# The last block of the last projection cut at columns 416 and 128, and the final norm's statistics and row scaling rearranged

## The chip, the cores and the metric

One core of a Trainium2 chip runs one launch of a hand-written program for five engines: TensorE (PE, with its weight loads PEld), VectorE (DVE), ScalarE (ACT), GpSimd (POOL) and SyncE (SP). The metric is the device time of one execution in microseconds, lower is better; the time shown is the median of several executions.

## The reference, cut to what matters

An encoder of four layers works on 512 prompt tokens and 32 sample tokens, 1024 features each. Each layer is a mixer (linear attention, band attention, a recurrent block) and a SwiGLU feed-forward network. The change touches the end alone: the second half of the last `w_out` product and the final norm.

```python
def rmsnorm(x, g):
    xf = x.astype(jnp.float32)
    y = xf * lax.rsqrt(jnp.mean(xf * xf, axis=-1, keepdims=True) + EPS)
    return (y * g.astype(jnp.float32)).astype(x.dtype)

def swiglu_ffn(x, w_in, w_out):
    g, u = jnp.split(x @ w_in, 2, axis=-1)
    return (jax.nn.silu(g) * u) @ w_out
...
        xp = xp + swiglu_ffn(rmsnorm(xp, ffn_norms[i]), *ffn_params[i])
        xs = xs + swiglu_ffn(rmsnorm(xs, ffn_norms[i]), *ffn_params[i])
    y_prompt = rmsnorm(xp, final_norm)
    y_sample = rmsnorm(xs, final_norm)
```

## The kernel before

Activations lie transposed in memory: `x` holds eight blocks (`XT` = 8) of 128 features by 544 tokens (`TOK`). Tokens 0 to 511 are the prompt, in four tiles of 128 (tiles 0 to 3), and the last 32 are the sample, tile `QT` = 4; the turn of tile 4 takes the last 128 columns and 32 rows of the result are used.

A projection makes one block of 128 output features at a time. For the last one, `down1` of layer 3, the contraction has 11 steps (`FH`), and each step is three matmuls (high times high, low times high, high times low halves of activations `h` and weights `w`), since products are split into two reduced-precision float32 parts (dtype fp32r). The name of a matmul in the rows is output, then activations and weights. Blocks 0 to 6 run in `mm_block` (lines 2378 in the rows), each matmul twice, on 272 columns. VectorE scales the block by `rstd` (L2052) and adds it to `x` (L2055); ScalarE squares it (L783) and makes a copy with the final gain, `xf` (L1236); GpSimd adds the squares into `sq_sum` (L2982); TensorE turns `xf` into token rows five tiles at a time (`end_turn`, L2337) and ScalarE copies these to `EN["rows"]` (L1219, L1220). Each of these is one block behind TensorE.

Block 7, the last, is computed in two token parts, `END_PARTS`: part 0 is columns 256 to 543 with tiles 2, 3 and 4, part 1 is columns 0 to 255 with tiles 0 and 1. TensorE's matmuls for both are at L2842 in `last_project`. For each part this chain follows:

- VectorE multiplies by `rstd` (L2059) and adds to `x` (L2062)
- ScalarE squares (L1425) and makes the copy with the gain (L1427)
- VectorE adds the squares to `sq_sum` (L2065)
- TensorE sums over the features with one matmul of one column for each tile (`end_sum`, L2860), then turns the tiles of block 7 (`end_turn_last`, L2337)
- ScalarE takes the root (L1430), VectorE the reciprocal (L2068)
- VectorE (L2074, L2076) and ScalarE (L1433, L1435) scale the rows of a tile: first 896 columns from `EN["rows"]`, then the last 128 from PSUM
- a DMA writes the tile's 128 rows of 1024 float32 (512 KB; the sample 128 KB)

Order is set by the order of the code on each engine and by semaphores; there is no scheduler. On TensorE `end_sum(0)` and `end_turn_last(0)` stand between the steps of part 1 (after steps 4 and 5). VectorE and ScalarE run all of part 0 and then all of part 1. SP issues the writes of tiles 2, 3, 4 and 0 (L735, L737, L739, L741), each behind its wait; ScalarE issues that of tile 1 last (L1438).

Of the kernel before, what the change touches and what calls it, by code (L numbers as in the profile page):

```python
# [24 lines left out]
ALU = mybir.AluOpType  # L25
# [156 lines left out]
def encoder_step(nc, d, o, layers=4):  # L182
# [15 lines left out]
    with ctx:  # L198
# [3 lines left out]
        def sem(name):  # L202
            return ctx.enter_context(nc.semaphore(name))
# [116 lines left out]
        def one(t, m, cols=slice(0, TOK), rows=slice(0, P)):  # L320
# [49 lines left out]
        s_eh, s_ea, s_esq, s_exf, s_esum, s_est, s_erms, s_einv, s_etn = (sem("end_part_" + n) for n in (  # L370
            "mm", "x", "square", "x_gain", "squares_summed", "mean_mm", "rms", "inv_rms", "turned"))
# [8 lines left out]
        END_PARTS = ((slice(2 * P, TOK), (2, 3, QT)), (slice(0, 2 * P), (0, 1)))  # L380
        END_LAST = (XT - 1) * P
        END_AT = {0: A0[:, 0:P], 2: A0[:, P:2 * P], QT: A0[:, 2 * P:3 * P], 1: A1[:, 0:P], 3: A1[:, P:2 * P]}
# [45 lines left out]
        def gain(name, m):  # L428
            return vec_a[:, ds(m + COL_A[name], 1)]
# [105 lines left out]
        def _(sp):  # L535
# [198 lines left out]
            sp.wait_ge(s_yd, 1)  # L734
            sp.dma_start(y_rows[:, 2:3, :], EN["rows"][:, 2:3, :]).then_inc(s_yo, 16)  # L735
            sp.wait_ge(s_ya, 1)
            sp.dma_start(y_rows[:, 3:4, :], EN["rows"][:, 3:4, :]).then_inc(s_yo, 16)  # L737
# [10 lines left out]
        def _(act):  # L748
# [672 lines left out]
            for c, (cols, tiles) in enumerate(END_PARTS):  # L1421
                t = tiles[1]
# [4 lines left out]
                act.activation(EN["xf"][1][:, cols], one(x, XT - 1, cols), ACT.Copy,  # L1427
                               scale=gain("final_norm", XT - 1)).then_inc(s_exf, 1)
                act.wait_ge(s_est, c + 1)
                act.activation(rms5[:, tiles[0]:tiles[-1] + 1], A2[:, 480 + tiles[0]:481 + tiles[-1]], ACT.Sqrt,  # L1430
                               bias=eps[:, 0:1]).then_inc(s_erms, 1)
                act.wait_ge(s_einv, c + 1)
                act.activation(EN["rows"][:, t, 0:END_LAST], EN["rows"][:, t, 0:END_LAST], ACT.Copy, scale=inv5[:, t:t + 1])  # L1433
                act.wait_ge(s_etn, c + 1)
                act.activation(EN["rows"][:, t, END_LAST:], END_AT[t], ACT.Copy,  # L1435
                               scale=inv5[:, t:t + 1]).then_inc(s_ya, 1)
            act.wait_ge(s_ya, 2)
            act.dma_start(y_rows[:, 1:2, :], EN["rows"][:, 1:2, :]).then_inc(s_yo, 16)  # L1438
# [5 lines left out]
        def _(dve):  # L1444
# [600 lines left out]
            def last_project(i, b0, kt):  # L2045
# [11 lines left out]
                for c, (cols, tiles) in enumerate(END_PARTS):  # L2057
# [12 lines left out]
                    dve.wait_ge(s_ye, m)  # L2070
                    for t in tiles[0:3:2]:
                        rows = ALL if t < QT else SAMPLE
                        inv = inv5[rows, t:t + 1]
                        dve.tensor_scalar(EN["rows"][rows, t, 0:END_LAST], EN["rows"][rows, t, 0:END_LAST], inv, None, ALU.mult)  # L2074
                        dve.wait_ge(s_etn, c + 1)
                        dve.tensor_scalar(EN["rows"][rows, t, END_LAST:], END_AT[t][rows, :], inv, None, ALU.mult).then_inc(s_yd, 1)  # L2076
# [256 lines left out]
        def _(pe):  # L2333
# [495 lines left out]
            def last_project(b0, q0):  # L2829
# [9 lines left out]
                for c, (cols, tiles) in enumerate(END_PARTS):  # L2839
                    for k in range(FH):  # L2840
# [14 lines left out]
            def end_sum(c):  # L2855

                pe.wait_ge(s_esum, c + 1)
                for t in END_PARTS[c][1]:
                    cols = slice(t * P, (t + 1) * P) if t < QT else slice(TOK - P, TOK)
                    ins = pe.matmul(A2[:, 480 + t:481 + t], sq_sum[:, cols], mean_x[:, 0:1], start=True, stop=True)  # L2860
                ins.then_inc(s_est, 1)

            def end_turn_last(c):

                pe.wait_ge(s_exf, c + 1)
                pe.wait_ge(s_ye, XT - 2)
# [244 lines left out]
```

## Time and profile before

| | us |
|---|---|
| median of 3 runs | 2536.77 (2536.25 to 2537.08) |
| profiled execution, its time | 2536.17 |
| its span, first to last event | 2534.4 |
| last block's first matmul, from the span's start | 2515.57 |
| last matmul of its part 1 starts | 2525.80 |
| first output write issued | 2525.04 |
| last output write issued | 2530.44 |

The page gives for each engine its busy share of the span; the chain of waits, followed back from the last event, gives what would have to be shorter for the end to come earlier. Times inside the trace count from the span's start. Only the last 19 us of the span belong to the code that the change touches.

### The profile page before, as it was taken

To read this page: it belongs to the slowest core of one execution; us is meant where nothing else is said; L and a number is where in the kernel's file an instruction comes from. 1 tells how busy PE (TensorE), PEld (TensorE's weight loads), DVE (VectorE), ACT (ScalarE), POOL (GpSimd) and SP (SyncE) were. 2 spreads that over 40 slices of the span, in tenths; PEclk is the share of its full clock that TensorE was granted. 3 is DMA by queue.
4 is the path that set the end of the run, shared out by engine and by line. 5 is a ranking of instruction groups with operands and counts; after the bars stand their busy time and mean duration, and the time that the engine had idled before them with its cause. 6 is when DMAs were issued, how large, how long until landed. Compare 5 with 4: busy or idle time off the path is not lost.

```text
span 2534.4 us, 48129 instructions
## 1 busy us (share of the span) xinstructions
PE 2516.1 (99%) x19925; PEld 2451.5 (97%) x19925; DVE 1747.4 (69%) x2578; ACT 1206.0 (48%) x1822; POOL 169.1 (7%) x180
## 2 busy tenths in 40 slices
PE   8999999999999999999999999999999999999998
PEld 8999999999988899999998899999999999999998
DVE  6555994984555599489557557948955565984973
ACT  5454651543555565245245545524534544642543
POOL 1101000001000010000122210000011101000001
PEclk9999999999999999999999999999999999999999
DMA  4222333332433233333222233332323223333332
GB/s 120 71 78 84 100 102 91 100 96 78 120 97 109 74 108 96 97 95 96 85 68 76 70 91 88 102 102 84 97 81 88 72 70 90 109 88 93 106 89 78
DMA packets 443890, 230.68 MB, mean 91 GB/s; under 512 B 17092, under 2 KB 440736, under 8 KB 443696
## 3 DMA queue, kind: packets, MB, share of 16 engines
q1 hardware_dynamic: 442048, 226.90, 31.2%
q8 instruction: 140, 2.29, 0.4%
q10 hardware_dynamic: 1200, 0.59, 0.1%
q0 software_dynamic: 448, 0.45, 0.1%
q14 instruction: 54, 0.44, 0.1%
HBM read 219.03 MB, written 8.87 MB: 90 GB/s over the span
## 4 chain that ended last, share of the span: by engine, by line
PE 96%; DVE 2%; ACT 1%; issue 1%; DMA 0%; SPq 0%; ACTq 0%; DVEq 0%
PE slot L2378 32%; PE slot L2421 21%; PE aux L2885 6%; PE aux L2880 6%; PE aux L2882 6%; PE slot L2885 5%; PE slot L2880 5%; PE slot L2882 5%; PE aux L2337 2%; PE aux L2783 1%; PE aux L2546 1%; PE aux L2789 1%; PE aux L2695 1%; PE aux L2633 1%; PE aux L2561 1%
## 5 line engine op out<-in xcount | busy, mean ns | idle before, releaser
L765 ACT ACTIVATE w_hi<-raw 128x1024 fp32r<-128x1024 f32 (+3 forms) x208 | 241.1, 1159 | 275.3 <-PE slot L2421 136.7
L2378 PE MATMUL slot<-xg_hi,w_hi 128*128 128x272 f32 x1664 | 361.4, 298 | 2.5 <-DVE w_lo L1462 1.5
L2378 PE MATMUL slot<-xg_lo,w_hi 128*128 128x272 f32 x1664 | 343.7, 288 | 0.0
L2378 PE MATMUL slot<-xg_hi,w_lo 128*128 128x272 f32 x1664 | 343.6, 288 | 0.0
L1462 DVE TENSOR_TENSOR w_lo<-raw,w_hi 128x1024 fp32r<-128x1024 f32 (+4 forms) x208 | 284.2, 1366 | 68.8 <-ACT w_hi L765 66.8
L2378 PEld LDWEIGHTS slot<-xg_hi,w_hi 128*128 128x128 f32 x1664 | 260.5, 189 | 14.2 <-issue 7.8
L2378 PEld LDWEIGHTS slot<-xg_lo,w_hi 128*128 128x128 f32 x1664 | 261.3, 188 | 0.0
L2378 PEld LDWEIGHTS slot<-xg_hi,w_lo 128*128 128x128 f32 x1664 | 260.3, 189 | 0.0
L2982 POOL TENSOR_TENSOR sq_sum<-sq_sum,sq_x 128x544 f32<-128x544 f32 x48 | 67.9, 1414 | 1609.8 <-ACT sq_x L783 1609.5
L2097 DVE TENSOR_TENSOR ffn_y<-slot,rstd 128x544 f32<-128x544 f32 x56 | 40.6, 725 | 193.9 <-PE slot L2421 177.7
L2421 PE MATMUL slot<-h_hi,w_hi 128*128 128x272 f32 x1078 | 150.0, 287 | 0.0
L2421 PE MATMUL slot<-h_hi,w_lo 128*128 128x272 f32 x1078 | 149.8, 287 | 0.0
L2421 PE MATMUL slot<-h_lo,w_hi 128*128 128x272 f32 x1078 | 149.8, 287 | 0.0
L783 ACT ACTIVATE sq_x<-x 128x544 f32<-128x544 f32 (+1 forms) x55 | 36.2, 657 | 223.0 <-DVE x L2100 119.4
L2421 PEld LDWEIGHTS slot<-h_hi,w_hi 128*128 128x128 f32 x1078 | 140.5, 188 | 0.0
L2421 PEld LDWEIGHTS slot<-h_lo,w_hi 128*128 128x128 f32 x1078 | 140.1, 188 | 0.0
L2421 PEld LDWEIGHTS slot<-h_hi,w_lo 128*128 128x128 f32 x1078 | 140.0, 188 | 0.0
L2885 PE MATMUL aux<-ffn_t_hi,w_lo 128*128 128x272 f32 x704 | 116.7, 287 | 0.0
L2880 PE MATMUL aux<-ffn_t_hi,w_hi 128*128 128x272 f32 x704 | 116.6, 287 | 0.0
L2882 PE MATMUL aux<-ffn_t_lo,w_hi 128*128 128x272 f32 x704 | 116.5, 287 | 0.0
L1290 ACT ACTIVATE w_hi<-ffn_w_sums 128x1024 fp32r<-128x1024 f32 x80 | 85.1, 1064 | 65.9 <-DVE ffn_w_sums L2134 64.8
L1308 ACT ACTIVATE w_hi<-ffn_w_sums 128x1024 fp32r<-128x1024 f32 x80 | 85.0, 1062 | 61.8 <-PE aux L2885 29.5
(406 smaller groups left out, 5757.4 us busy)
## 6 DMA issues: line engine op xcount, KB each, us to landing
raw<-in_l_ffn_w_out_dram SPq DMA_DIRECT2D x64, 704.0 KB, 4.7
raw<-in_l_ffn_w_in_dram SPq DMA_DIRECT2D x52, 512.0 KB, 5.0
raw<-in_l_gla_w_in_dram SPq DMA_DIRECT2D x47, 512.0 KB, 3.9
ffn_raw_b<-in_l_ffn_w_in_dram SPq DMA_DIRECT2D x88, 256.0 KB, 3.4
ffn_raw_b<-in_l_ffn_w_in_dram SPq DMA_DIRECT2D x44, 512.0 KB, 5.2
raw<-in_l_ffn_w_in_dram SPq DMA_DIRECT2D x72, 256.0 KB, 3.4
raw<-in_l_att_w_qkv_dram SPq DMA_DIRECT2D x24, 512.0 KB, 3.8
raw<-in_l_lru_w_in_dram SPq DMA_DIRECT2D x24, 512.0 KB, 3.9
```

The costliest lines, as they stand in the source:

```text
L765: act.activation(w_hi[par][:, 0:kt, :], raw[par][:, 0:kt, :], ACT.Copy).then_inc(s_hi, 1)
L1290: act.activation(tiles8(w_his, w_slots(b % 2)[0]), tiles8(FF["s"], 0), ACT.Copy).then_inc(s_wh, 1)
L1308: act.activation(tiles8(w_his, min(w_slots(b % 2)[2:4])), tiles8(FF["s"], 2 * KQ), ACT.Copy).then_inc(s_wh, 1)
L1462: dve.tensor_tensor(w_lo[par][:, 0:kt, :], raw[par][:, 0:kt, :], w_hi[par][:, 0:kt, :].bitcast(F32), ALU.subtract).then_inc(s_lo, 1)
L2097: dve.tensor_tensor(FF["y"][:, 2 * j:2 * j + 2, :], slot[(p0 + j) % 2][:, :, 0:HALF], halves(rstd[:, :]), ALU.mult).then_inc(s_free, 1)
L2337: return pe.transpose(out, in_, ident[rows, rows])
L2378: ins = pe.matmul((slot[par] if bank is None else bank)[:, hf, 0:HALF], w[par][:, k, :], a[:, k0 + k, hf * HALF:(hf + 1) * HALF], start=(k ...
L2421: ins = pe.matmul(to[:, hf, 0:HALF], w[par][:, k, :], a[:, k, cols], start=(k == 0 and at == 0), stop=(k == kt - 1 and at == 2))
L2880: pe.matmul(to, w_his[:, w_at + k, :], hi(k), start=(start and k == 0), stop=False, skip_group_check=True)
L2882: pe.matmul(to, w_his[:, w_at + k, :], lo(k), start=False, stop=False, skip_group_check=True)
L2885: ins = pe.matmul(to, w_los[:, w_at + k, :], hi(k), start=False, stop=(stop and k == KQ - 1), skip_group_check=True)
L2982: pool.tensor_tensor(sq_sum[:, :], sq_sum[:, :], sq_x[par][:, :], ALU.add).then_inc(s_xad, 1)
```

## The change

`END_PARTS` becomes part 0 = columns 128 to 543 with tiles 1, 2, 3 and 4, and part 1 = columns 0 to 127 with tile 0. VectorE's addition of the squares goes; `end_sum` makes two accumulating matmuls for a tile, one on `sq_sum` and one on the block's squares `sq_x[1]`. On TensorE `end_sum(0)` and `end_turn_last(0)` move from between the steps of part 1 to behind them. VectorE runs the add of part 1 right after the reciprocal of part 0, and then scales tiles 1 and 4, takes part 1's reciprocal, and scales tile 0. ScalarE scales the front of tile 2, squares part 1, finishes tile 2, takes part 1's root and scales tile 3. SP writes tiles 1, 2, 4 and 0, ScalarE tile 3.

```diff
-        END_PARTS = ((slice(2 * P, TOK), (2, 3, QT)), (slice(0, 2 * P), (0, 1)))
+        END_PARTS = ((slice(P, TOK), (1, 2, 3, QT)), (slice(0, P), (0,)))
...
             sp.wait_ge(s_yd, 1)
+            sp.dma_start(y_rows[:, 1:2, :], EN["rows"][:, 1:2, :]).then_inc(s_yo, 16)
+            sp.wait_ge(s_ya, 1)
             sp.dma_start(y_rows[:, 2:3, :], EN["rows"][:, 2:3, :]).then_inc(s_yo, 16)
-            sp.wait_ge(s_ya, 1)
-            sp.dma_start(y_rows[:, 3:4, :], EN["rows"][:, 3:4, :]).then_inc(s_yo, 16)
...
+            end_square(0)
+            end_root(0)
+            act.wait_ge(s_einv, 1)
+            end_front(2)
+            end_square(1)
+            act.wait_ge(s_etn, 1)
+            end_back(2)
+            end_root(1)
+            end_front(3)
+            end_back(3)
             act.wait_ge(s_ya, 2)
-            act.dma_start(y_rows[:, 1:2, :], EN["rows"][:, 1:2, :]).then_inc(s_yo, 16)
+            act.dma_start(y_rows[:, 3:4, :], EN["rows"][:, 3:4, :]).then_inc(s_yo, 16)
...
-                    dve.wait_ge(s_esq, c + 1)
-                    dve.wait_ge(s_xad, (XT - 2) * stat_of["final"])
-                    dve.tensor_tensor(sq_sum[:, cols], sq_sum[:, cols], sq_x[m % 2][:, cols], ALU.add).then_inc(s_esum, 1)
...
+                end_add(0)
+                end_inverse(0)
+                end_add(1)
+                dve.wait_ge(s_ye, m)
+                end_rows(0, 1)
+                end_rows(0, QT)
+                end_inverse(1)
+                end_rows(1, 0)
...
-                        if c and k == 4:
-                            end_sum(0)
-                        if c and k == 5:
-                            end_turn_last(0)
+                end_sum(0)
+                end_turn_last(0)
                 end_sum(1)
                 end_turn_last(1)

             def end_sum(c):

-                pe.wait_ge(s_esum, c + 1)
+                pe.wait_ge(s_xad, (XT - 2) * stat_of["final"])
+                pe.wait_ge(s_esq, c + 1)
                 for t in END_PARTS[c][1]:
                     cols = slice(t * P, (t + 1) * P) if t < QT else slice(TOK - P, TOK)
-                    ins = pe.matmul(A2[:, 480 + t:481 + t], sq_sum[:, cols], mean_x[:, 0:1], start=True, stop=True)
+                    pe.matmul(A2[:, 480 + t:481 + t], sq_sum[:, cols], mean_x[:, 0:1], start=True, stop=False)
+                    ins = pe.matmul(A2[:, 480 + t:481 + t], sq_x[1][:, cols], mean_x[:, 0:1], start=False, stop=True)
                 ins.then_inc(s_est, 1)
```

TensorE before, inside part 1 (L2842 are its steps, L2860 the sums of part 0 over the features, L2337 the turns of part 0's tiles):

```order
L2842 MATMUL slot<-h_hi,w_hi 128x256
L2842 MATMUL slot<-h_lo,w_hi 128x256
L2842 MATMUL slot<-h_hi,w_lo 128x256
L2860 MATMUL aux<-mean_x,sq_sum 128x1 [waits end_part_squares_summed]
L2860 MATMUL aux<-mean_x,sq_sum 128x1 x2
L2842 MATMUL slot<-h_hi,w_hi 128x256
L2842 MATMUL slot<-h_lo,w_hi 128x256
L2842 MATMUL slot<-h_hi,w_lo 128x256
L2337 MATMUL aux<-ident,end_xf 128x128 [waits end_rows,end_part_x_gain]
L2337 MATMUL aux<-ident,end_xf 128x128 x2
```

TensorE of the change, from the last matmul of part 1 on (now L2873, with 128 columns; the sums are L2890 and L2891, the turns L2368):

```order
L2873 MATMUL slot<-h_hi,w_lo 128x128
L2890 MATMUL aux<-mean_x,sq_sum 128x1 [waits end_part_square,square_added]
L2891 MATMUL aux<-mean_x,sq_x 128x1
L2890 MATMUL aux<-mean_x,sq_sum 128x1
L2891 MATMUL aux<-mean_x,sq_x 128x1
L2890 MATMUL aux<-mean_x,sq_sum 128x1
L2891 MATMUL aux<-mean_x,sq_x 128x1
L2890 MATMUL aux<-mean_x,sq_sum 128x1
L2891 MATMUL aux<-mean_x,sq_x 128x1
L2368 MATMUL aux<-ident,end_xf 128x128 [waits end_rows,end_part_x_gain]
L2368 MATMUL aux<-ident,end_xf 128x128 x3
```

Part 0's sums are now eight matmuls where there were three, and stand behind all of part 1's matmuls instead of in their middle; part 1's sums follow behind the turns.

VectorE before, part 0 from its reciprocal on and then part 1:

```order
L2068 RECIPROCAL inv<-rms 128x3 [waits end_part_rms]
L2074 TENSOR_SCALAR end_rows<-end_rows,inv 128x896 [waits end_rows,end_part_inv_rms]
L2076 TENSOR_SCALAR end_rows<-aux,inv 128x128 [waits end_part_turned]
L2074 TENSOR_SCALAR end_rows<-end_rows,inv 32x896
L2076 TENSOR_SCALAR end_rows<-aux,inv 32x128 [waits end_part_turned]
L2059 TENSOR_TENSOR ffn_y<-slot,rstd 128x256 [waits end_part_mm]
L2062 TENSOR_TENSOR x<-ffn_y,x 128x256 [waits block_read]
L2065 TENSOR_TENSOR sq_sum<-sq_sum,sq_x 128x256 [waits square_added,end_part_square]
L2068 RECIPROCAL inv<-rms 128x2 [waits end_part_rms]
L2074 TENSOR_SCALAR end_rows<-end_rows,inv 128x896 [waits end_rows,end_part_inv_rms]
L2076 TENSOR_SCALAR end_rows<-aux,inv 128x128 [waits end_part_turned]
```

VectorE of the change, the same stretch:

```order
L2090 RECIPROCAL inv<-rms 128x4 [waits end_part_rms]
L2080 TENSOR_TENSOR ffn_y<-slot,rstd 128x128 [waits end_part_mm,end_part_inv_rms]
L2083 TENSOR_TENSOR x<-ffn_y,x 128x128 [waits block_read]
L2097 TENSOR_SCALAR end_rows<-end_rows,inv 128x896 [waits end_rows]
L2099 TENSOR_SCALAR end_rows<-aux,inv 128x128 [waits end_part_turned]
L2097 TENSOR_SCALAR end_rows<-end_rows,inv 32x896
L2099 TENSOR_SCALAR end_rows<-aux,inv 32x128 [waits end_part_turned]
L2090 RECIPROCAL inv<-rms 128x1 [waits end_part_rms]
L2097 TENSOR_SCALAR end_rows<-end_rows,inv 128x896 [waits end_part_inv_rms]
L2099 TENSOR_SCALAR end_rows<-aux,inv 128x128 [waits end_part_turned]
```

Part 1's multiply and add moved ahead of all row scaling, and stand behind the reciprocal of part 0; the addition of squares is gone.

ScalarE before, and then of the change, from part 0's root on:

```order
L1430 ACTIVATE rms<-aux,eps 128x3 [waits end_part_mean_mm]
L1433 ACTIVATE end_rows<-end_rows,inv 128x896 [waits end_part_inv_rms]
L1435 ACTIVATE end_rows<-aux,inv 128x128 [waits end_part_turned]
L1425 ACTIVATE sq_x<-x 128x256 [waits square_added,end_part_x]
L1427 ACTIVATE end_xf<-x,vec_a 128x256 [waits end_turned]
L1430 ACTIVATE rms<-aux,eps 128x2 [waits end_part_mean_mm]
L1433 ACTIVATE end_rows<-end_rows,inv 128x896 [waits end_part_inv_rms]
L1435 ACTIVATE end_rows<-aux,inv 128x128 [waits end_part_turned]
L1438 DMA out_dram<-end_rows 128x1024 [waits end_scaled_act]
```

The same of the change:

```order
L1435 ACTIVATE rms<-aux,eps 128x4 [waits end_part_mean_mm]
L1440 ACTIVATE end_rows<-end_rows,inv 128x896 [waits end_part_inv_rms]
L1426 ACTIVATE sq_x<-x 128x128 [waits square_added,end_part_x]
L1428 ACTIVATE end_xf<-x,vec_a 128x128 [waits end_turned]
L1444 ACTIVATE end_rows<-aux,inv 128x128 [waits end_part_turned]
L1435 ACTIVATE rms<-aux,eps 128x1 [waits end_part_mean_mm]
L1440 ACTIVATE end_rows<-end_rows,inv 128x896
L1444 ACTIVATE end_rows<-aux,inv 128x128
L1456 DMA out_dram<-end_rows 128x1024 [waits end_scaled_act]
```

Part 1's square and gained copy moved between the two pieces of the first tile's scaling, ahead of the wait for that tile's turn.

## Rows read from the trace of the kernel before

**Rows 1.** The page's chain that ended last: its shares by engine.

```profile
PE 96%; DVE 2%; ACT 1%; issue 1%; DMA 0%; SPq 0%; ACTq 0%; DVEq 0%
```

**Rows 2.** Chain of waits, last 35 us: start us, us, what.

```profile
2504.68 8.26 PE slot L2378 x66
...
2515.73 3.20 PE slot L2842 x24
2518.93 0.55 PE aux L2337 x5
...
2520.71 0.47 DVE ffn_y L2059
...
2522.17 0.47 DVE sq_sum L2065
...
2522.68 0.84 PE aux L2860 x6
...
2523.55 0.28 ACT rms L1430
...
2524.06 0.69 DVE end_rows L2074
...
2526.13 0.44 DVE ffn_y L2059
...
2527.98 0.62 PE aux L2860 x4
...
2529.11 1.04 ACT end_rows L1433
2530.16 0.26 ACT end_rows L1435
```

**Rows 3.** Timeline of TensorE in the last block: start, duration, instruction.

```profile
2515.57 0.29 PE L2842 MATMUL slot<-h_hi,w_hi 128*128 128x288 f32 x1
...
2520.51 0.28 PE L2842 MATMUL slot<-h_hi,w_hi 128*128 128x256 f32 x1
...
2523.83 0.49 PE L2337 MATMUL aux<-ident,end_xf 128*128 128x128 f32 x3
...
2524.28 0.28 PE L2842 MATMUL slot<-h_lo,w_hi 128*128 128x256 f32 x1
...
2525.80 0.28 PE L2842 MATMUL slot<-h_hi,w_lo 128*128 128x256 f32 x1
```

**Rows 4.** Groups by shape, 2490 to 2535 us: busy us, mean ns.

```profile
L2052 DVE TENSOR_TENSOR ffn_y<-slot,rstd 128x544 f32<-128x544 f32 x4 | 2.9, 725 | 12.2 <-PE slot L2378 12.2
...
L2059 DVE TENSOR_TENSOR ffn_y<-slot,rstd 128x256 f32<-128x256 f32 x1 | 0.4, 425 | 0.0
...
L783 ACT ACTIVATE sq_x<-x 128x544 f32<-128x544 f32 x4 | 2.6, 658 | 11.5 <-DVE x L2055 11.5
...
L1427 ACT ACTIVATE end_xf<-x,vec_a 128x256 f32<-128x256 f32 x1 | 0.5, 492 | 0.0
...
L1425 ACT ACTIVATE sq_x<-x 128x256 f32<-128x256 f32 x1 | 0.4, 416 | 1.7 <-DVE x L2062 1.7
```

**Rows 5.** Timeline of the output writes' issue: start, duration, queue.

```profile
2525.04 0.36 SPq L735 DMA_DIRECT2D out_dram<-end_rows  x1
...
2530.09 0.34 SPq L741 DMA_DIRECT2D out_dram<-end_rows  x1
2530.44 0.36 ACTq L1438 DMA_DIRECT2D out_dram<-end_rows  x1
```

**Rows 6.** Stretches at the end: engines' busy us, clock share, DMA share, GB/s.

```profile
2530.00:2531.00 1.00, 0.00 (x0) 0.00 (x0) 0.06 (x1) 0.41 (x2) 0.00 (x0) 0.64 0.10 41
2531.00:2532.00 1.00, 0.00 (x0) 0.00 (x0) 0.00 (x0) 0.00 (x0) 0.00 (x0) 0.50 1.00 401
2532.00:2533.00 1.00, 0.00 (x0) 0.00 (x0) 0.00 (x0) 0.00 (x0) 0.00 (x0) 0.50 1.02 401
2533.00:2534.00 1.00, 0.00 (x0) 0.00 (x0) 0.00 (x0) 0.00 (x0) 0.00 (x0) 0.50 0.53 205
```

More of the change, by code:

```diff
@@ L369, in encoder_step @@
             "end_x_gain", "end_turned", "end_rows", "end_scaled_dve", "end_scaled_act", "y_out"))
-        s_eh, s_ea, s_esq, s_exf, s_esum, s_est, s_erms, s_einv, s_etn = (sem("end_part_" + n) for n in (
-            "mm", "x", "square", "x_gain", "squares_summed", "mean_mm", "rms", "inv_rms", "turned"))
+        s_eh, s_ea, s_esq, s_exf, s_est, s_erms, s_einv, s_etn = (sem("end_part_" + n) for n in (
+            "mm", "x", "square", "x_gain", "mean_mm", "rms", "inv_rms", "turned"))
         s_hp = sem("head_square")
@@ L379, in encoder_step @@
         END_BANKS = ((A3, A2), (A0, A1))
[L380 removed]
+        END_PARTS = ((slice(P, TOK), (1, 2, 3, QT)), (slice(0, P), (0,)))
         END_LAST = (XT - 1) * P
[L382 removed]
+        END_AT = {0: A3[:, 0:P], 1: A0[:, 0:P], QT: A0[:, P:2 * P], 2: A1[:, 0:P], 3: A1[:, P:2 * P]}
         SCORE_BANK = (A0, A1)
@@ L1420, in _, with end_square @@
             n, y_rows = stat_of["final"] - 1, o[0].rearrange("a (t p) n -> (a p) t n", p=P)
-            for c, (cols, tiles) in enumerate(END_PARTS):
-                t = tiles[1]
+            def end_square(c):
+                cols = END_PARTS[c][0]
                 act.wait_ge(s_ea, c + 1)
@@ L1428, in _, with end_root @@
                                scale=gain("final_norm", XT - 1)).then_inc(s_exf, 1)
+            def end_root(c):
+                tiles = END_PARTS[c][1]
                 act.wait_ge(s_est, c + 1)
@@ L1431, in _, with end_front, end_back @@
                                bias=eps[:, 0:1]).then_inc(s_erms, 1)
-                act.wait_ge(s_einv, c + 1)
+            def end_front(t):
                 act.activation(EN["rows"][:, t, 0:END_LAST], EN["rows"][:, t, 0:END_LAST], ACT.Copy, scale=inv5[:, t:t + 1])
-                act.wait_ge(s_etn, c + 1)
-                act.activation(EN["rows"][:, t, END_LAST:], END_AT[t], ACT.Copy,
-                               scale=inv5[:, t:t + 1]).then_inc(s_ya, 1)
+            def end_back(t):
+                act.activation(EN["rows"][:, t, END_LAST:], END_AT[t], ACT.Copy, scale=inv5[:, t:t + 1]).then_inc(s_ya, 1)
+            end_square(0)
[8 more added lines that the diff above has]
+            end_back(3)
             act.wait_ge(s_ya, 2)
-            act.dma_start(y_rows[:, 1:2, :], EN["rows"][:, 1:2, :]).then_inc(s_yo, 16)
+            act.dma_start(y_rows[:, 3:4, :], EN["rows"][:, 3:4, :]).then_inc(s_yo, 16)
         @block.vector
@@ L2056, in last_project, with end_add @@
                 m = XT - 1
-                for c, (cols, tiles) in enumerate(END_PARTS):
+                def end_add(c):
+                    cols = END_PARTS[c][0]
                     dve.wait_ge(s_eh, c + 1)
@@ L2062, in last_project, with end_inverse @@
                     dve.tensor_tensor(one(x, m, cols), FF["u"][:, cols], one(x, m, cols), ALU.add).then_inc(s_ea, 1)
-                    dve.wait_ge(s_esq, c + 1)
-                    dve.wait_ge(s_xad, (XT - 2) * stat_of["final"])
-                    dve.tensor_tensor(sq_sum[:, cols], sq_sum[:, cols], sq_x[m % 2][:, cols], ALU.add).then_inc(s_esum, 1)
+                def end_inverse(c):
+                    tiles = END_PARTS[c][1]
                     part = slice(tiles[0], tiles[-1] + 1)
@@ L2069, in last_project, with end_rows @@
                     dve.wait_ge(s_einv, c + 1)
[L2070 to L2076, printed above, removed]
+                def end_rows(c, t):
+                    rows = ALL if t < QT else SAMPLE
+                    inv = inv5[rows, t:t + 1]
+                    dve.tensor_scalar(EN["rows"][rows, t, 0:END_LAST], EN["rows"][rows, t, 0:END_LAST], inv, None, ALU.mult)
+                    dve.wait_ge(s_etn, c + 1)
+                    dve.tensor_scalar(EN["rows"][rows, t, END_LAST:], END_AT[t][rows, :], inv, None, ALU.mult).then_inc(s_yd, 1)
+                end_add(0)
[6 more added lines that the diff above has]
+                end_rows(1, 0)
             def project_out(i, name, b0, kt):
@@ L2865, in end_turn_last @@
                 pe.wait_ge(s_exf, c + 1)
-                pe.wait_ge(s_ye, XT - 2)
+                pe.wait_ge(s_ye, XT - 2 + c)
                 for t in END_PARTS[c][1]:
```

## Prediction

> **What bounds the kernel now.** First the chain by engine [rows 1]: TensorE is 96% of it, so nothing off TensorE matters until the last block. Then the chain of waits in the last 35 us [rows 2], which is where the whole change lies: the reader sees TensorE's steps, then from 2520.71 us on a relay of short pieces through VectorE, ScalarE and TensorE, once for part 0 and, from 2526.13, once for part 1, to 2530.42 (2530.16 + 0.26). Nothing in it overlaps. Then TensorE's timeline for the pace of single matmuls [rows 3], the groups by shape for how an operation's time grows with columns [rows 4], the issue times of the writes [rows 5], and the stretches at the end [rows 6]. The last shows what the chain of waits leaves out: from 2531 to 2533.5 the core does nothing but write output, at 401 GB/s with the DMA engines busy 1.00 of the time. The bandwidth of the write is the last limit, and how much is still unwritten when the last chain closes decides the end.
>
> How far the end lies behind the last data: 41 + 401 + 401 + 205 is 1.05 MB, which is the two tiles issued at 2530.09 and 2530.44 [rows 5, 6]. So data flowed from about 2530.90 (41/401 of a microsecond before 2531), 0.81 us behind the first issue, to about 2533.51 (205/401 of one behind 2533), and the span of 2534.4 ends 0.89 us later. The three other pieces (1.18 MB) were issued from 2525.04 on and had 5 us beside the chain of part 1 to drain.
>
> **TensorE, part 0: 416 columns instead of 288.** The paces in the rows are 24 matmuls of 288 columns in 3.20 us (0.133), 66 of 272 in 8.26 us (0.125) [rows 2], and 13 steps of 256 columns from 2524.28 to 2525.80 (0.117) [rows 3]. In proportion, 416 columns take 0.193; by the slope from 256 to 288 (0.5 ns for a column) 0.197; I take 0.193. 33 x (0.193 - 0.133) is +1.98 us. The turn of block 6 inside the part (0.55 [rows 2]) stays. So the multiply of part 0 moves from 2520.71 to about 2522.70, and part 1's first matmul from 2520.51 [rows 3] to 2522.49.
>
> **TensorE, part 1: 128 columns instead of 256.** No row has a fp32r matmul of 128 columns. Every matmul has its own weight load, and the nearest rows for what lies under it are the sums and the turns: the sums move one column, and 6 records take 0.84 and 4 take 0.62 us [rows 2], 0.11 for each more; the turns move 128 columns, 5 take 0.71 - the first 0.27 of it is one matmul's own length - and 3 take 0.49 [rows 3], again 0.11. Halving the columns of a one-column or a 128-column matmul buys nothing; I read 0.112 as the floor that the weight load sets. Bounds: half of 0.117, which is 0.058, if no load binds; two records of 0.112, which is 0.224, if a narrow fp32r matmul runs as the sums do (see below). I take 0.112, since fp32r and plain float32 loads have the same 128x128 weights. 33 x 0.112 = 3.70 us, and part 1 ends at 2522.49 + 3.70 = 2526.19. Before, the last matmul of part 1 started at 2525.80, with part 0's sums and turns already inside.
>
> The Trainium skill, "TensorE: Matmul & The Clock Gate", section "LDWEIGHTS (loading the stationary operand)", makes a weight load cost its columns divided by 1.2 in ns, an estimate of 107 ns for 128. The rows' 0.11 agrees, and by the page's value the sum would be 0.2 us less. What this rule says against the change: a matmul with fewer columns than its weight load hides costs its load, so cutting off a small part does not make that part cheap.
>
> **The squares.** VectorE's addition goes (0.47 of part 0's chain [rows 2], and as much in part 1's). In its place each sum has two matmuls. A sum of three tiles shows as 6 records [rows 2], two for each matmul, so part 0 now has 4 tiles x 2 x 2 = 16 records and part 1 has 4. The root followed the first record by 0.87 (2522.68 to 2523.55) with 6 and by 0.64 with 4; 16 give 0.64 + 12 x 0.112 = 1.98.
>
> **Where the sums stand.** Part 0's chain: multiply and add at 0.59 each (725 ns at 544 columns, 425 at 256, so 1.04 ns a column [rows 4]), square 0.55 (658 and 416 ns), hand-overs 0.03 each: the squares are ready at 2522.70 + 0.59 + 0.03 + 0.59 + 0.03 + 0.55 = 2524.49. Nobody takes them: TensorE is in part 1 until 2526.19. That is a wait of 1.7 us that before did not exist, since the sums stood inside part 1. The square and the gained copy are hidden by it, and so is the saved addition of part 0. Then root at 2526.19 + 1.98 = 2528.17, and from the root to the scaling 0.51 (2523.55 to 2524.06 [rows 2]): 2528.68. Before, part 0 reached this point at 2524.06: 4.6 us earlier.
>
> **Who is queued behind.** Part 1's multiply and add (0.29 each, the same line through 725 and 425) stand behind part 0's reciprocal on VectorE, though TensorE has finished part 1 at 2526.2. They run from 2528.68 to 2529.32. ScalarE is in tile 2's front from 2528.68 (1.04 [rows 2], next start 0.95 later), so the square of part 1 starts at 2529.63 and takes 0.31. TensorE's sum of part 1 starts at 2529.98, its root at 2530.62, tile 3's front at 2530.90, its back piece 0.95 later, and that ends 0.35 later: tile 3 is issued by ScalarE at about 2532.22. The gained copy (492 ns at 256 columns, about 0.39 here) and the back of tile 2 fill ScalarE until the root and cost nothing more; tile 2 is ready at about 2530.5.
> VectorE: tile 1 from 2529.34, issued 0.98 later (2524.06 to 2525.04 [rows 2, 5]) at 2530.32; the sample 1.09 later at 2531.41 (2525.04 to 2526.13); reciprocal 0.21; tile 0 issued at 2532.60.
>
> **The sum.** The last issue moves from 2530.44 to 2532.60. The first moves from 2525.04 to 2530.32, and this is what costs more: all 2.23 MB are written behind it. Data from 2530.32 + 0.81 = 2531.13, 2.23 / 0.401 = 5.56 us, to 2536.69, span end 0.89 later: 2537.6, which is +3.2. The queues don't run dry, since all is issued and flowing by 2533.4 while the first four pieces (1.70 MB) last until 2535.4. The profiled execution took 2536.17, 1.8 over its span, so 2539.4 on that scale; it lay 0.6 under the median of the runs, and on the median the forecast is 2536.77 + 3.2 = 2540.0 us.
>
> The rate of 401 GB/s is from a write alone [rows 6]. The Trainium skill, "DMA: Bandwidth & Descriptors", section "Where 436 GB/s comes from", gives about 358 GB/s as the memory's limit for one core. The trace is above that, and the measurement decides; at 358 the sum would be 0.7 us more.
>
> **Rivals.**
> - *Narrow matmuls run at their columns.* If weights loaded faster than I read, part 1's matmuls would take 0.058 each, 1.78 us less in all: part 1 ends at 2524.41, just when the squares are ready. All later steps move up by 1.7, the write stays the limit, and the median is 2538.3. Against it: sums of one column at 0.11 [rows 2]. The Trainium skill, "TensorE: Matmul & The Clock Gate", section "Weight-path perf modes — Fast Weight Load (FWL) and DoubleRow", has a fast load for 128 weights that are not FP32, and does not say which fp32r is.
> - *Slower: narrow fp32r matmuls take two passes.* If a matmul of 128 columns at fp32r costs two records as the sums do, 33 x 0.224 = 7.4 us instead of 3.7. All behind it moves: +6.9, 2543.7. For it: no fp32r matmul under 256 columns is in the rows. Against it: fp32r shows one record a matmul everywhere. It decides "slower" from a pace of 0.17 on, where 33 x 0.058 = 1.9 carries +3.2 over the bound of 5.1; load and columns in a row (0.112 + 0.058) would just reach that, but the turns show them overlapped.
> - *The order of writes hides.* If the queues had drained when tile 0 is issued at 2532.60, only its 0.52 MB (1.31 us) would stand behind it: 2532.60 + 0.81 + 1.31 + 0.89 = 2535.6, median 2538.0. That needs 1.70 MB in 2.3 us, 0.74 MB a microsecond, and the rows show 0.401.
> - *The change does what its parts suggest:* a shorter second chain and an earlier end. Part 1's chain itself is shorter (0.29 for 0.43 twice, no addition, a smaller square), by about 0.9 us. It could show only if part 0's output had left before, which needs its sums ahead of part 1's end. For faster by 0.2% the first write would have to be issued about 8 us earlier than worked out. I see nothing for that.
>
> **How the numbers follow.** My forecast 2540.0 has 0.74, fast loads 0.13, two passes 0.08, drained queues 0.03, a gain 0.02. 0.2% of 2536.77 is 5.1 us, about what a measurement of this kernel can tell from no change: from 2541.9 on it is slower. The range 2538.0 to 2541.8 holds the first two cases and the fourth, with the spread of the write rate (0.7) and of the wide pace (0.004 x 33, 0.1) and 1 us for what was strung together from 20 pieces. Slower 0.10 (two passes, and a pace near 0.17), faster 0.02, within 0.88.
>
> **What would show it.** Right: part 0 at 0.19 a matmul and part 1 at 0.11; TensorE's sums (L2890) starting at once behind the last L2873, at about 2526.2, with 16 records; VectorE idle from 2523.9 to 2528.5, then reciprocal, then part 1's multiply; the first write issued at about 2530.3 and the DMA share at 1.00 for 5.5 us to the end. Wrong: a pace of 0.06 or over 0.15 in part 1; the root of part 0 before 2527; a gap in the writes between 2531.2 and 2536.7; or a change in the time of anything ahead of 2515.57, which the forecast takes as untouched.

## The result, and the profile after

| | before | after |
|---|---|---|
| median, us | 2536.46 (2535.75 to 2537.13, 20 runs) | 2540.02 (2539.50 to 2540.86, 20 runs) |
| profiled execution, its time | 2536.17 | 2540.41 |
| its span | 2534.4 | 2538.7 |
| last block's first matmul | 2515.57 | 2516.20 |
| first write issued, behind that matmul | +9.47 | +14.45 |
| last write issued | +14.87 | +16.92 |
| data flowing | to +18.13 | +15.30 to +21.60 |
| end of the span | +18.87 | +22.47 |

The ratio is 1.0015, with a 95% interval of 1.0009 to 1.002: 3.6 us slower, outside what the runs' spread explains, but under the 0.2% (5.1 us) that was called "no change" ahead of the run. The two traces start the last block 0.63 us apart, through two steps of about 0.3 us in code that the change does not touch; 20 runs of the kernel before spread over 1.4 us. So all that follows counts from the last block's first matmul, written +x. On that scale the trace moves by 3.60 us, and the medians by 3.56.

The chain by engine of the page of after answers [rows 1]. It looks the same and tells nothing of the change:

```profile
PE 96%; DVE 2%; issue 1%; ACT 1%; DMA 0%; DVEq 0%; SPq 0%; ACTq 0%
```

The chain of waits of after, its last 24 us (start us, us, what), answers [rows 2]. Both parts' matmuls now stand in it as one block; the sums over the features are eight pieces in a row; and part 1's sum is a second group:

```profile
2516.36 4.60 PE slot L2873 x24
2520.97 0.55 PE aux L2368 x5
2521.51 5.35 PE slot L2873 x42
2526.86 0.17 PE aux L2890 x2
2527.03 0.22 PE aux L2891 x2
...
2528.63 0.28 ACT rms L1435
...
2528.93 0.19 DVE inv L2090
...
2530.53 0.56 PE aux L2890 x2
2531.09 0.44 PE aux L2891 x2
```

The timeline of after (start, duration, engine, line, operation; in brackets the idle time before and what ended it) answers [rows 3] and [rows 5]:

```profile
2516.97 0.35 PE L2873 MATMUL slot<-h_lo,w_hi 128*128 128x416 f32 x1
...
2523.24 0.28 PE L2873 MATMUL slot<-h_hi,w_lo 128*128 128x128 f32 x1
...
2526.59 0.27 PE L2873 MATMUL slot<-h_hi,w_lo 128*128 128x128 f32 x1
2526.70 0.33 PE L2890 MATMUL aux<-mean_x,sq_sum 128*128 128x1 f32 x2
...
2528.63 0.27 ACT L1435 ACTIVATE rms<-aux,eps 128x4 f32<-128x4 f32 x1 [3.03 <-PE aux L2891]
...
2529.14 0.29 DVE L2080 TENSOR_TENSOR ffn_y<-slot,rstd 128x128 f32<-128x128 f32 x1
...
2530.53 0.56 PE L2890 MATMUL aux<-mean_x,sq_sum 128*128 128x1 f32 x2 [1.44 <-ACT sq_x L1426]
...
2530.65 0.36 SPq L735 DMA_DIRECT2D out_dram<-end_rows  x1
...
2533.03 0.39 ACTq L1456 DMA_DIRECT2D out_dram<-end_rows  x1
2533.12 0.39 SPq L741 DMA_DIRECT2D out_dram<-end_rows  x1
```

From 2523.24 to 2526.59 stand 30 steps of 0.112 us. The sums start right behind the last step, 0.11 later, though the squares have been ready since 2525.07. ScalarE had been idle 3.03 us when the root came.

The stretches at the end of after (each engine's busy us, granted clock, DMA share, GB/s) answer [rows 6]:

```profile
2530.00:2531.00 1.00, 0.47 (x3) 0.50 (x3) 0.97 (x3) 0.93 (x4) 0.00 (x0) 0.50 0.00 0
2531.00:2532.00 1.00, 0.83 (x4) 0.54 (x4) 0.85 (x3) 0.45 (x2) 0.00 (x0) 0.50 0.55 221
2532.00:2533.00 1.00, 0.00 (x0) 0.00 (x0) 0.95 (x3) 1.00 (x2) 0.00 (x0) 0.50 1.00 397
2533.00:2534.00 1.00, 0.00 (x0) 0.00 (x0) 0.09 (x1) 0.00 (x1) 0.00 (x0) 0.50 1.03 389
2534.00:2535.00 1.00, 0.00 (x0) 0.00 (x0) 0.00 (x0) 0.00 (x0) 0.00 (x0) 0.50 1.02 201
2535.00:2536.00 1.00, 0.00 (x0) 0.00 (x0) 0.00 (x0) 0.00 (x0) 0.00 (x0) 0.50 0.97 393
2536.00:2537.00 1.00, 0.00 (x0) 0.00 (x0) 0.00 (x0) 0.00 (x0) 0.00 (x0) 0.50 1.02 418
2537.00:2538.00 1.00, 0.00 (x0) 0.00 (x0) 0.00 (x0) 0.00 (x0) 0.00 (x0) 0.50 0.52 209
```

Nothing is written before 2531, and then one stretch carries all 2.23 MB without a gap. All of it is issued by 2533.51, over four microseconds before the data ends. One slice, 2534 to 2535, moves only 201 GB/s with the DMA engines busy 1.02 of the time; the prediction did not have that.

### The profile page after: what moved, and what is told of

It is laid out like the page before. It is cut to its first block, busy times and chain, and to the rows that moved or that the text cites. A ratio compares the mean times of both kernels' runs of the same rounds, so it can differ in the third digit from the quotient of the medians.

```text
span 2538.7 us, 48146 instructions
## 1 busy us (share of the span) xinstructions
PE 2519.0 (99%) x19935; PEld 2454.2 (97%) x19935; DVE 1746.7 (69%) x2576; ACT 1205.7 (47%) x1822; POOL 169.0 (7%) x180
## 4 chain that ended last, share of the span: by engine, by line
PE 96%; DVE 2%; issue 1%; ACT 1%; DMA 0%; DVEq 0%; SPq 0%; ACTq 0%
PE slot L2409 32%; PE slot L2452 21%; PE aux L2916 6%; PE aux L2911 6%; PE aux L2913 6%; PE slot L2916 5%; PE slot L2911 5%; PE slot L2913 5%; PE aux L2368 2%; PE aux L2814 1%; PE aux L2577 1%; PE aux L2820 1%; PE aux L2726 1%; PE aux L2664 1%; PE aux L2592 1%
```

## The experiments

Eleven runs of each kernel give its median; each is set against the kernel before, run beside it on the same chip (2536.21, 2536.21 and 2536.28 us in the three sets of runs). The changed kernel ran again with the third set:

> The changed kernel once more, beside the others of this study. Expected 3.4 to 3.6 us over the kernel before. From the last block's first matmul to the span's end 22.5 us (within 0.2), whatever comes ahead of it. If the granted clock falls at another point than 13.4 us behind that matmul, as it did in the kernels without a write, the sums of part 0 and with them the first write shift, and the end with them.

It gave 2539.68 us (ratio 1.0013, 1.0004 to 1.0022), with its first write at +14.48 and its end at +22.49. The trace of after repeats within 0.03 us, and 2539.68 is what the variants of the changed kernel are compared with.

The theory: what is unwritten when the first write is issued, at the bandwidth of the write, sets the end. The rivals: the last issue sets it; TensorE's place for the sums does; or the accumulating matmuls do.

### The sums back inside part 1

```diff
-                end_sum(0)
-                end_turn_last(0)
+                        if c and k == 5:
+                            end_sum(0)
+                        if c and k == 6:
+                            end_turn_last(0)
```

> The changed kernel, with the sums and turns of part 0 put back inside TensorE's part 1 (behind steps 5 and 6); VectorE and ScalarE keep their new order. Theory (the first write decides, and it stands behind part 1's multiply and add on VectorE): part 0's root comes about 1.5 us earlier (2.05 us behind step 5's end instead of behind the whole part), but part 1 ends 1.8 + 0.4 us later, so part 1's multiply, and the first write behind it, stay within 0.2 us of where they were: 2540.1 us, no gain. Rival (the place of the sums alone cost the time): first write and end 1.5 us earlier, 2538.5.

> The kernel with the sums of part 0 inside part 1 once more; its 11 times spread over 3.1 us (the changed kernel's over 1.4) with a median of 2541.1, 1.5 over the one that was profiled. Theory: in the slow ones TensorE's granted clock falls within part 1, behind the 16 one-column records, and what is left of part 1 runs at half the pace, and part 1's multiply and the first write wait for it. Expected again a spread over 2.5 us, and in the profile, if its time is over 2540.5, part 1's last matmul later than 12.86 us behind the first of the block, with the clock at 0.50 before it. Rival (something else in the run spreads): the same tail as in the first profile, with a later start of the block.

Timeline of the first of the two:

```profile
2525.61 0.36 PE L2893 MATMUL aux<-mean_x,sq_x 128*128 128x1 f32 x2
2526.01 0.27 ACT L1435 ACTIVATE rms<-aux,eps 128x4 f32<-128x4 f32 x1 [1.56 <-PE aux L2893]
...
2528.43 0.29 DVE L2080 TENSOR_TENSOR ffn_y<-slot,rstd 128x128 f32<-128x128 f32 x1 [1.94 <-PE slot L2873]
...
2529.93 0.36 SPq L735 DMA_DIRECT2D out_dram<-end_rows  x1
```

The root of part 0 comes 1.46 us earlier (+10.97 for +12.43), and nothing is won: VectorE's next instruction is part 1's multiply, it now waits 1.94 us for TensorE, and it starts at +13.39 where it stood at +12.94. The first write is issued at +14.89 (second time +14.69), and the end comes at +22.81 (+22.61). The second of the two is 0.20 earlier in all of this because of the clock, as the last section says. So the late sums are no loss by themselves as long as part 1's multiply and add stand ahead of the rows.

The medians are 2541.1 (2539.62 to 2542.68) and 2540.27 (2539.54 to 2542.38). This spread of 3 us is not in the changed kernel (2539.14 to 2540.21), and both profiled executions lie at the low end of their range. So the 0.6 to 1.4 us by which their medians lie over the changed kernel's have no trace; see the last section.

### The same, and the rows of part 0 ahead of part 1's add

VectorE scales tiles 1 and 4 before it takes up part 1, ScalarE scales tiles 2 and 3 and issues tile 3 before it squares part 1. Beside the edit above, and the like on ScalarE (left out here):

```diff
...
                 end_inverse(0)
-                end_add(1)
                 end_rows(0, 1)
                 end_rows(0, QT)
+                end_add(1)
                 end_inverse(1)
```

> As the kernel with the sums inside, and in addition VectorE scales tiles 1 and 4 ahead of part 1's multiply and add, and ScalarE finishes tiles 2 and 3 and issues tile 3 ahead of part 1's square. Theory (write bandwidth behind the first issue): first write issued 2.0 us earlier than in the changed kernel, tile 0 issued last at about the same time as there; all data flow without a gap, so the end is 2.0 us earlier: 2538.0. Rival (the last issue decides): tile 0's issue is between 0.3 us earlier and unchanged, so 2539.7 to 2540.0.

Timeline of its writes:

```profile
2528.01 0.36 SPq L735 DMA_DIRECT2D out_dram<-end_rows  x1
2528.42 0.42 SPq L737 DMA_DIRECT2D out_dram<-end_rows  x1
2529.10 0.58 SPq L739 DMA_DIRECT2D out_dram<-end_rows  x1
...
2529.55 0.35 ACTq L1454 DMA_DIRECT2D out_dram<-end_rows  x1
...
2532.95 0.34 SPq L741 DMA_DIRECT2D out_dram<-end_rows  x1
```

The first issue is 2.0 us earlier than in the changed kernel (+12.45), the last one 0.48 later (+17.40 for +16.92), and the end 2.07 earlier (+20.40). The median is 2537.73 (2537.03 to 2539.72; ratio 1.0006, 0.9997 to 1.0015), 1.95 under the changed kernel. First and last issue moved in opposite directions, and the end went with the first. This is the largest piece of the 3.6 us. It is also about as far as an earlier first write can help: tile 0, issued at +17.40, has its first data at +18.24, when tile 3's last data (+18.37) are nearly out, and the stream thins to about 215 GB/s from +17.85 to +18.25. From here on the last issue counts too. The rows ahead of part 1's add without the sums inside part 1 were not run, so the 2.0 us can't be divided between the two edits.

### Less to write

Tile 1's 512 KB are not written in the first kernel, the sample's 128 KB in the second:

```diff
-            sp.dma_start(y_rows[:, 1:2, :], EN["rows"][:, 1:2, :]).then_inc(s_yo, 16)
...
-            sp.wait_ge(s_yo, 16 * 5)
+            sp.wait_ge(s_yo, 16 * 4)
```

```diff
-            sp.dma_start(o[1][0], EN["rows"][SAMPLE, QT, :]).then_inc(s_yo, 16)
...
-            sp.wait_ge(s_yo, 16 * 5)
+            sp.wait_ge(s_yo, 16 * 4)
```

> The changed kernel without the write of tile 1 (512 KB, the first of the five; its rows are not in the output). Theory (write bandwidth): data start 0.4 us later with tile 2 and are 0.52 MB less, 1.3 us at 401 GB/s, so the end comes 0.9 to 1.0 us earlier: 2539.1. Rival (the last issue and a fixed time behind it decide): nothing changes, 2540.0.

> The changed kernel without the write of the sample (128 KB in 32 rows; it is not in the output). Theory as I had it (each byte at 401 GB/s): 0.33 us less, 2539.7. Second theory (the stretch at 201 GB/s in the trace of the changed kernel is this write): 0.8 us less, 2539.2, and no slow stretch is left. Rival (last issue decides): 2540.0.

Without tile 1 the median is 2538.67, 1.0 less, and the trace ends at +21.11, 1.38 less, though its last issue stands at +16.82, where it hardly moved (+16.96). Its first issue is 0.32 later (tile 2 at +14.80) and 0.52 MB less flow behind it (1.3 us at 0.401): 1.0 less. That speaks for bandwidth again.

Without the sample, stretches of the trace:

```profile
2532.00:2533.00 1.00, 0.00 (x0) 0.00 (x0) 0.62 (x2) 0.54 (x2) 0.00 (x0) 0.50 1.03 418
2533.00:2534.00 1.00, 0.00 (x0) 0.00 (x0) 0.00 (x0) 0.00 (x0) 0.00 (x0) 0.50 1.02 393
2534.00:2535.00 1.00, 0.00 (x0) 0.00 (x0) 0.00 (x0) 0.00 (x0) 0.00 (x0) 0.50 1.00 410
2535.00:2536.00 1.00, 0.00 (x0) 0.00 (x0) 0.00 (x0) 0.00 (x0) 0.00 (x0) 0.50 1.01 393
```

The slice of 201 GB/s is gone. The data takes 5.36 us for 2.10 MB, against 6.32 for 2.23: the sample costs 0.96 us of the stretch, where 0.13 MB at 0.401 would be 0.33. The median fell less, by 0.43 to 2539.25 (2537.87 to 2539.68). In the profiled execution the end came at +22.06, because its first write was issued 0.61 late; the last section says why. So the sample's price is 0.96 against the changed kernel's trace, and the whole kernel showed 0.4 of it.

### The last sum at full clock

Eleven matmuls of 272 columns, into a PSUM buffer that nobody reads any more, in front of part 1's sum:

```diff
                 end_turn_last(0)
+                pe.wait_ge(s_free, b)
+                for k in range(11):
+                    pe.matmul(slot[1 - par][:, 0, 0:HALF], w_hi[par][:, k, :], FF["h_hi"][:, k, 0:HALF], start=True, stop=True)
                 end_sum(1)
```

> The changed kernel with eleven matmuls whose result nobody reads on TensorE between part 0's turns and part 1's sum, where it was idle and its granted clock fell. Theory (write bandwidth): part 1's sum runs at the full clock, four records in 0.45 instead of 0.85 us, its root and the last write's issue come 0.3 to 0.4 us earlier, and the end doesn't move: 2540.0. Rival (the last chain decides): 0.35 us earlier, 2539.65.

The wanted condition did not come about as meant. The clock had already fallen to 0.50 at 2527.35, inside part 0's sums, and rose again at 2530.77, when most of the added matmuls were over; part 1's sum itself ran at full clock (0.54 us to its root where the changed kernel took 1.02), but started later:

```profile
2531.16 0.28 PE L2893 MATMUL aux<-mean_x,sq_sum 128*128 128x1 f32 x2
...
2531.70 0.26 ACT L1435 ACTIVATE rms<-aux,eps 128x1 f32<-128x1 f32 x1 [1.16 <-PE aux L2894]
```

It still answers another question: the root of part 1 came at +16.23 instead of +15.35, the last issue at +17.80 instead of +16.92, and the end at +22.53 instead of +22.47. The median is 2539.62 (ratio 1.0013, 1.0004 to 1.0022), that of the changed kernel. So the last issue has at least 0.9 us to spare. But it did not move alone: the first write was 0.34 later too, and by the theory that should have moved the end as much. The end stayed because the data took 6.01 us here, where the six other traces of the new order that write all 2.23 MB have 6.30 to 6.35. What shortened them is not shown; the slice from 2534 to 2535, with the end of the sample's write, moved 324 GB/s, where in after the slowest slice moved 201.

### VectorE adds part 0's squares again

`end_squares(0)` puts the removed addition back for part 0 alone, behind its add; the sum of part 0 is one matmul for a tile again:

```diff
                 end_add(0)
+                end_squares(0)
                 end_inverse(0)
...
-                    pe.matmul(A2[:, 480 + t:481 + t], sq_sum[:, cols], mean_x[:, 0:1], start=True, stop=False)
...
+                    ins = pe.matmul(A2[:, 480 + t:481 + t], sq_sum[:, cols], mean_x[:, 0:1], start=True, stop=c == 0)
```

> The changed kernel with VectorE's addition of part 0's squares put back (part 1 stays with accumulating matmuls). Theory: the addition (0.6 us) is hidden, since TensorE is in part 1 then; the sums have 8 records for 16, so root, first write and end come 0.9 us earlier: 2.6 us over the kernel before, 2539.1. Rival (the 16 records cost nothing, since the sums wait for something else): unchanged, 3.5 over.

Timeline:

```profile
2526.00 1.00 PE L2901 MATMUL aux<-mean_x,sq_sum 128*128 128x1 f32 x8
...
2527.04 0.27 ACT L1435 ACTIVATE rms<-aux,eps 128x4 f32<-128x4 f32 x1 [2.13 <-PE aux L2901]
...
2529.05 0.36 SPq L735 DMA_DIRECT2D out_dram<-end_rows  x1
```

Eight records where after has 16; the root at +11.54 for +12.43; the first write at +13.55 for +14.45; the end at +21.47, 1.0 less. The median is 2538.84 (ratio 1.001, 1.0001 to 1.0019), 0.84 less. In this order the addition would cost nothing, since VectorE waits anyway, and the matmuls in its place cost 0.9. First and last issue both moved by 0.9 to 1.0 here, so this run prices the matmuls but does not tell which issue sets the end.

### The accumulating matmuls alone, in the kernel before

The squares' addition goes, as in the change, and nothing else is altered (the edit of `end_sum` is that of the change):

```diff
...
-                    dve.tensor_tensor(sq_sum[:, cols], sq_sum[:, cols], sq_x[m % 2][:, cols], ALU.add).then_inc(s_esum, 1)
...
```

> The kernel before with one part of the change alone: the squares are summed by accumulating matmuls instead of VectorE's addition; parts of 288 and 256 columns and the old order stay. Theory: part 0's sum starts 0.25 us earlier and has 12 records for 6 (+0.67), so TensorE ends part 1 0.4 us later and part 1's chain starts 0.4 later; in that chain the addition (-0.47) and 4 more records (+0.45) cancel: +0.35 us, 2536.8. Rival (taking VectorE's addition off the chain is a gain): 2536.0 or less.

2536.36 us, 0.15 more than before, its end at +19.16 for +18.87 (ratio 1.0001, 0.9992 to 1.001). A gain is not there; whether it is a loss, this run can't tell. In part 1's chain four more records (0.45) take the place of an addition of 0.47; in part 0 six more push part 1's multiply 0.25 later (+10.81 for +10.56).

### Versions of the kernel before that could be quicker

For part 1 alone, TensorE sums `sq_sum` while it would wait anyway, and adds the new squares when they come; part 0 keeps VectorE's addition:

```diff
...
-                end_sum(1)
+                pe.wait_ge(s_erms, 1)
+                for src, first in ((sq_sum, True), (sq_x[1], False)):
+                    if not first:
+                        pe.wait_ge(s_esq, 2)
+                    for t in END_PARTS[1][1]:
+                        ins = pe.matmul(A2[:, 480 + t:481 + t], src[:, t * P:(t + 1) * P], mean_x[:, 0:1],
+                                        start=(first and t == END_PARTS[1][1][0]), stop=not first, skip_group_check=True)
```

> The kernel before, with accumulating matmuls for part 1 alone, and their first half (on the sums of blocks 0 to 6) ahead of the wait, where TensorE is idle from 2526.1 to 2528.0. Theory: the addition and its hand-over (0.47) leave part 1's chain, the added matmuls are hidden, both last writes are issued 0.47 us earlier, and since the queues are empty by then the end moves as much: 2536.0. Rival (nothing but the rate of the writes counts): unchanged, 2536.5.

The second kernel also writes tile 0 in two halves, the first as soon as its 512 columns are scaled (VectorE's side of it is left out):

```diff
-            sp.dma_start(y_rows[:, 0:1, :], EN["rows"][:, 0:1, :]).then_inc(s_yo, 16)
+            sp.dma_start(y_rows[:, 0:1, 0:SEQ], EN["rows"][:, 0:1, 0:SEQ]).then_inc(s_yo, 16)
+            sp.wait_ge(s_yd, 4)
+            sp.dma_start(y_rows[:, 0:1, SEQ:2 * SEQ], EN["rows"][:, 0:1, SEQ:2 * SEQ]).then_inc(s_yo, 16)
...
```

> As the one with part 1's first matmuls early, and in addition tile 0 is scaled and written in two pieces: 512 columns first, then the rest, so the first data of the last pair start earlier. Theory (what counts is when the last stretch of writing starts): its first issue comes about 0.5 us earlier still, so 2535.5. Rival (rows of 2 KB are written less efficiently, or the second piece comes too late to keep the queue full): 2536.0, no gain over the one before.

The third halves tile 1's write and scaling in the same way:

> The kernel before with part 1's first sums early and tile 0 written in two pieces (2535.4), and in addition tile 1 written in two pieces too, the first issued by SyncE as soon as ScalarE has its first 512 columns. Theory: the gap in the writes behind tile 0's first piece (57 GB/s in a quarter of a microsecond) closes, 0.2 us earlier: 2535.2, 1.0 under the kernel before. Rival (more pieces cost more than the gap): 2535.4 or more.

Timeline of the second kernel, which has the early sum of the first too:

```profile
2526.17 0.50 PE L2863 MATMUL aux<-mean_x,sq_sum 128*128 128x1 f32 x4
...
2527.76 0.61 PE L2863 MATMUL aux<-mean_x,sq_x 128*128 128x1 f32 x4 [1.08 <-ACT sq_x L1427]
...
2529.41 0.34 SPq L741 DMA_DIRECT2D out_dram<-end_rows  x1
2530.00 0.33 SPq L743 DMA_DIRECT2D out_dram<-end_rows  x1
2530.22 0.36 ACTq L1440 DMA_DIRECT2D out_dram<-end_rows  x1
```

The four records of `sq_sum` stand in time that TensorE had free (it then idles 1.08 us), and only four are left behind the square. Medians: 2535.78 for the early sum (0.43 under its before, end at +18.42), 2535.38 with the halved write (0.83 under, end at +18.04), 2535.7 with both halved (0.58 under, end at +18.12). The 2535.2 expected of the third was missed; halving tile 1 too won nothing. In the kernel before the write had drained when the last chain closed, so there, unlike in the changed kernel, an earlier last issue does count. The second is the quickest kernel of this study, but by 0.03%: its ratio is 0.9997, with an interval of 0.9988 to 1.0006, so a gain is not shown beyond doubt; its highest run (2535.81) lies barely over the lowest of the kernel before (2535.68).

## Why the prediction was right, point by point

| step, behind the first matmul | predicted | measured |
|---|---|---|
| 416-column matmul, us | 0.193 | 0.191 |
| part 0's multiply | +7.13 | +7.07 |
| 128-column matmul, us | 0.112 | 0.112 |
| sums of part 0 start | +10.62 | +10.50 |
| root of part 0 | +12.60 | +12.43 |
| multiply of part 1 | +13.11 | +12.94 |
| first write issued | +14.75 | +14.45 |
| root of part 1 | +15.05 | +15.35 |
| last write issued | +17.03 | +16.92 |
| data, us | 5.56 | 6.30 |
| last data to end, us | 0.89 | 0.87 |
| end | +22.03 | +22.47 |

- **What bounds the kernel.** The bandwidth of the write behind the first issue, as the stretches said. Two runs show it outright: the first issue earlier and the last later (end 2.07 earlier), and less data behind an almost unmoved last issue (1.38 earlier). The run with eleven extra matmuls shows that the last issue has room (0.88 later, end 0.06 later), but not that the first decides to the tenth: it moved by 0.34 there and the end did not follow. From the first issue to the end the six other traces of the new order with all data have 7.92 to 8.02 us, and that run 7.74; from the last issue to the end the same traces have anything from 3.00 to 5.55. This step carried the forecast; a reading that followed the chain of waits alone would have ended at the last issue and given +2.2.
- **The paces.** Both right within 0.003 us. That the weight load sets the narrow one is a reading: the pace is that of a record of the one-column sums (0.11), and no run changed the load. The rivals that hung on it, fast loads (0.058) and two passes (0.224), are both refuted by 30 steps at 0.112. (The 0.71 for five turns, given with rows 3, is not among the rows shown; the timeline of before has it.)
- **The sums behind part 1.** Right in place and size: 16 records, 1.93 us from first record to root for 1.98. That they do harm *there* was only half of the step, as the first experiment shows: moved back inside, they win nothing until the rows of part 0 also go ahead of part 1's add. Both together cost 2.0.
- **The removed addition.** The text said that the wait hides it, so that its removal saves nothing, and counted the added records on the path. The run with VectorE's addition put back confirms both, at 0.84 for the 0.9 of eight records.
- **The mis-sized term: the time of the data**, 5.56 for 6.30. "2.23 / 0.401" took one rate for all of it; the sample's write lowers it for about a microsecond, and without it the data ran at 391 GB/s over its whole stretch (2.10 MB in 5.36 us). The trace of the kernel before has the same in the stretch that the prediction did not look at, where the sample went out behind tiles 2 and 3:

```profile
2528.00:2529.00 1.00, 0.86 (x6) 0.62 (x6) 0.09 (x1) 0.26 (x1) 0.00 (x0) 1.00 1.06 311
```

There 1.18 MB took 3.34 us, from +10.32 to +13.66, 0.4 more than at 0.401. The size of this miss also depends on where data are taken to end. The prediction took it from bytes (205/401 of a slice); by the last packet the data of before end 0.19 later (+18.13), 0.74 ahead of the span's end and not 0.89. Counted in the prediction's way, after has 6.07 us of data and 1.15 to the end.
- **Root of part 1.** Predicted with 0.64 from first record to root, measured 1.02: the granted clock was 0.50 by then, and the pairs came 0.42 apart. By the theory it cost nothing, since tile 0 waits for its place in the write anyway.
- **The number.** The move was 3.6 for 3.2. The chain up to the first write came 0.3 us early and the data took 0.74 longer; these two misses partly cancel. The rest of the exact agreement with 2540.0 is luck: the median of 20 runs of the kernel before is 0.3 under the median of three from which the forecast starts.
- **The rivals.** Drained queues: no gap in the data of after. A shorter second chain and a gain: refuted, the first write is 5.0 us later.

Of the 3.6 us, about 2.0 are the place of the sums and of the rows, taken together, and 0.9 are the accumulating matmuls, each measured on the changed kernel. The two need not add up, since with the sums inside part 1 their length weighs differently. The remainder, about 0.7, was not measured by itself; the wider part 0 with four tiles' output behind its chain is what is left of the change. No run has the new parts with the old orders of the engines.

## What to carry to other kernels

At the end of a kernel count the bytes that are still unwritten when the first output is issued: at 0.4 MB/us they can outlast every chain behind it, and then an earlier first write is worth more than a shorter last chain. Work that moves off an engine that waits saves nothing, and costs its full length on the engine that is waited for; put the part of it that depends on nothing new into that engine's own idle time instead. A narrow part is not cheap on TensorE: at 128 columns a matmul takes 0.112 us, at 256 it takes 0.117.

## What the runs showed of the hardware

**The clock fell while TensorE was busy.** In the run without the sample's write, stretches (the first number behind the five engines is the granted clock) and timeline:

```profile
2525.00:2526.00 1.00, 1.00 (x11) 1.00 (x11) 0.00 (x0) 0.00 (x0) 0.00 (x0) 1.00 0.00 0
2526.00:2527.00 1.00, 1.00 (x10) 1.00 (x9) 0.00 (x0) 0.00 (x0) 0.00 (x0) 0.83 0.00 0
2527.00:2528.00 1.00, 1.00 (x7) 1.00 (x6) 0.00 (x0) 0.00 (x0) 0.00 (x0) 0.50 0.00 0
```

```profile
2525.60 0.33 PE L2889 MATMUL aux<-mean_x,sq_sum 128*128 128x1 f32 x2
...
2526.71 0.57 PE L2890 MATMUL aux<-mean_x,sq_x 128*128 128x1 f32 x2
2527.14 0.57 PE L2889 MATMUL aux<-mean_x,sq_sum 128*128 128x1 f32 x2
```

The engine is busy 1.00 throughout and leaves no gap, but from 2525.60 on it issues one-column matmuls, and 128-column ones before. At 2526.66, 1.06 us into them, the granted clock goes from 1.00 to 0.50 (2.4 to 1.2 GHz), and a pair takes 0.43 instead of 0.22. That put part 0's root at +13.07 for +12.43. The run with eleven extra matmuls shows the same, at 2527.35. In after itself the clock fell at 2529.64, behind the sums, and in its second trace at +12.22, inside them but near their end, at a cost of 0.03. So what the sums of part 0 cost differs from execution to execution. With the sums inside part 1 a fall slows part 1's matmuls too, and the two traces of that kernel show a small case. In the first the clock fell at +12.71, within the last but one matmul of part 1, and part 1's multiply came at +13.39; in the second it fell at +13.14, behind the last one, and the multiply came at +13.19. First write and end are 0.20 apart in the same way. An earlier fall may be behind the wide spread of the three measurements with the sums inside part 1 (2.7 to 3.1 us between lowest and highest, where the changed kernel has 1.1 to 1.4). No trace of one of their longer executions exists, so that stays open.

**The sample's write is slow for its size.** 128 KB from 32 rows took 0.96 us of the stretch in after, where its bytes alone would be 0.33, with the DMA share at 1.02 and 201 GB/s in its slice. With the 6.01 us of the run with eleven extra matmuls it is 0.65, and in before the three pieces with the sample took 0.57 more than the two tiles behind them (3.34 for 2.77). The Trainium skill, "SBUF — State Buffer", section "Door 1: The DMA port swizzle (why `[64,N]` ≈ `[32,N]`)", says that a transfer's bandwidth depends on how many of 16 ports its partitions reach. The sample's rows are partitions 96 to 127, which by its table reach eight. As an estimate by that rule, half the rate for these bytes makes 0.65 us; the traces have 0.57 to 0.96. No run here moved the sample to other partitions, so the cause is not shown.
